# Modulation rows made inside the two expert loops, 512 columns per six tiles, instead of in the first stage, the merges, a projection and a feed-forward

## The reference, cut to what matters

```python
def first_block(...):
    c_act = jax.nn.silu(c)
    for l in range(2):
        mod = c_act @ ada_w[l] + ada_b[l]              # (D) @ (D, 6 D)
        sh_mix, sc_mix, g_mix, sh_ffn, sc_ffn, g_ffn = jnp.split(mod, 6, axis=-1)
        u = modulate(x, sh_mix, sc_mix)                # layer_norm(x) * (1 + sc) + sh
        ...                                            # w_in, four branches, gates
        x = layer_norm(DN_ALPHA * x + g_mix[:, None, :] * y, ln1_g[l], ln1_b[l])
        u = modulate(x, sh_ffn, sc_ffn)
        y = peer_ffn(u, ...)                           # the experts
        x = layer_norm(DN_ALPHA * x + g_ffn[:, None, :] * y, ln2_g[l], ln2_b[l])

def second_block(...):                                 # the same with c_2, ada_w_2, ada_b_2
    x = x + g_m * mixer(rms_norm(x) * (1 + sc_m) + sh_m)
    x = x + g_f * conv_ffn(rms_norm(x) * (1 + sc_f) + sh_f)
```

## Time and profile before

| what | value |
|---|---|
| device time, median of 3 runs | 4388.18 us (4385.45 to 4395.09) |
| profiled execution, span from first to last instruction | 4393.7 us |
| busy share of the span: PE, DVE, ACT, POOL | 79%, 62%, 42%, 4% |
| read from HBM | 633.94 MB, 145 GB/s over the span |
| mean granted PE clock | 0.896 |
| the two expert stages | 723.5 us each |
| the two merges | 188.5 us each |
| mod0 | 95.3 us |
| ffn_0 and ffn_1 | 267.2 and 207.7 us |

### The profile page before, as it was taken

How to read it: one execution, slowest core, us unless ns; L and a number is a source line. 1 busy time by engine, 2 the same in 40 slices (tenths; PEclk the granted TensorE clock), 3 DMA queues, 4 the chain that set the end, 5 groups by cost and what they waited for, 6 DMA issues and landing times. The chain is left out here.

```text
span 4393.7 us, 65322 instructions
## 1 busy us (share of the span) xinstructions
PE 3463.6 (79%) x20016; PEld 3012.6 (69%) x20016; DVE 2703.8 (62%) x5202; ACT 1834.7 (42%) x3304; POOL 154.6 (4%) x110
## 2 busy tenths in 40 slices
PE   1867865599999978678646999999674688796698
PEld 0846644589999968466445899999654577584587
DVE  6745648966666668456489666666634498344466
ACT  0433321755555544333218555555421234343244
POOL 0010000000000000100000000000003023000000
PEclk7978977899999989789778999999887799897799
DMA  7813621045555548136210455555410366451143
GB/s 257 277 51 106 218 99 57 19 148 188 185 190 187 186 154 268 52 116 225 90 48 19 158 187 186 190 188 185 174 52 25 135 235 215 143 184 34 55 180 129
DMA packets 279728, 636.50 MB, mean 145 GB/s; under 512 B 37896, under 2 KB 138896, under 8 KB 273472
## 3 DMA queue, kind: packets, MB, share of 16 engines
q1 hardware_dynamic: 279616, 635.15, 42.0%
HBM read 633.94 MB, written 1.15 MB: 145 GB/s over the span
## 5 line engine op out<-in xcount | busy, mean ns | idle before, releaser
L125 DVE TENSOR_TENSOR experts_u_lo<-u_w,experts_u_hi 128x512 fp32r<-128x512 f32 x512 | 353.8, 692 | 379.8 <-ACT experts_u_hi L122 379.8
L130 PE MATMUL experts_ps_h<-uP_hi,experts_u_hi 128*128 128x256 f32 x2048 | 576.9, 282 | 6.9 <-DVE experts_u_lo L125 6.9
L132 PE MATMUL experts_ps_h<-uP_hi,experts_u_lo 128*128 128x256 f32 x2048 | 574.5, 281 | 0.0
L131 PE MATMUL experts_ps_h<-uP_lo,experts_u_hi 128*128 128x256 f32 x2048 | 574.3, 280 | 0.0
L122 ACT ACTIVATE experts_u_hi<-u_w 128x512 fp32r<-128x512 f32 x512 | 323.1, 632 | 404.8 <-PE experts_ps_h L132 261.9
L125 DVE TENSOR_TENSOR experts_v_lo<-v_w,experts_v_hi 128x512 fp32r<-128x512 f32 x512 | 354.5, 692 | 179.8 <-ACT experts_v_hi L122 179.8
L122 ACT ACTIVATE experts_v_hi<-v_w 128x512 fp32r<-128x512 f32 x512 | 323.8, 632 | 233.2 <-PE expert_y L132 233.2
L130 PE MATMUL expert_y<-experts_v_hi,experts_w_hi 128*128 128x512 f32 x1024 | 405.2, 396 | 3.0 <-DVE experts_w_lo L125 3.0
L132 PE MATMUL expert_y<-experts_v_hi,experts_w_lo 128*128 128x512 f32 x1024 | 400.9, 391 | 0.0
L130 PEld LDWEIGHTS experts_ps_h<-uP_hi,experts_u_hi 128*128 128x128 f32 x2048 | 386.9, 189 | 17.1 <-issue 7.2
L131 PE MATMUL expert_y<-experts_v_lo,experts_w_hi 128*128 128x512 f32 x1024 | 397.9, 389 | 0.0
(11 more groups left out here) (516 smaller groups left out, 7614.3 us busy)
## 6 DMA issues: line engine op xcount, KB each, us to landing
u_w<-in_peer_u SPq DMA_DIRECT2D x256, 512.0 KB, 4.5
v_w<-in_peer_v SPq DMA_DIRECT2D x256, 512.0 KB, 3.3
up_w<-in_ffn_w_up SPq DMA_DIRECT2D x44, 1024.0 KB, 7.2
od_in_w<-in_od_w_in SPq DMA_DIRECT2D x36, 1024.0 KB, 5.1
in_w<-in_w_in SPq DMA_DIRECT2D x48, 752.0 KB, 5.4
merge_w_w<-in_w_gate SPq DMA_DIRECT2D x32, 1024.0 KB, 5.2
mod_mod_w<-in_ada_w_all SPq DMA_DIRECT2D x16, 1536.0 KB
in_proj_mod_w<-in_ada_w_all SPq DMA_DIRECT2D x24, 1024.0 KB
```

Of the source, the lines that this page charges most:

```text
L125: return dve.tensor_tensor(self.lo[at], value, self.hi[at].bitcast(F32), ALU.subtract)
L130: pe.matmul(out, left.hi[left_at], right.hi[right_at], start=start, stop=False, skip_group_check=skip)
L131: pe.matmul(out, left.hi[left_at], right.lo[right_at], start=False, stop=False, skip_group_check=skip)
L132: return pe.matmul(out, left.lo[left_at], right.hi[right_at], start=False, stop=stop, skip_group_check=skip)
```

## The change

The modulation rows are made elsewhere. Of row 0, `mod0` makes only the first 2048 columns, shift and scale of the mixer; the silu of both condition vectors is computed there once. `in_proj` of block 0 makes the next 3072 columns of row 0, as it made half of row 1 before. All else is made by a new class, `SpreadModulation`, in the two `experts` stages, in units of 512 columns. A unit takes six tiles: in each of the first four SP loads two chunks of 128 x 512 (512 KB) ahead of the tile's u load, and DVE adds the two chunks after the tile's own steps; in the fifth PE sums over the partitions; in the sixth ACT copies the row and stores it, from ACT's queue. The first `experts` stage makes 20 units (the last 1024 columns of row 0, all of row 1, half of row 3), the second 18 (row 2, the other half of row 3). `merge`, `in_proj` of block 1 and `ffn_0` make none; in `ffn_0` the low parts of the down weights are DVE's, as they were in `ffn_1`.

To know the row at build time, the loop over l is written out, so every stage of blocks 0 and 1 has its own code. The expert loop is unrolled by six tiles in place of two, in three hardware loops. Each norm loads and turns only its own 2048 columns, so the second norm of each block now does so as well. The gates are no longer loaded in the norms: `Residual`, `turn_project_add` and `conv_ffn` each load the one gate they use (512 KB) in their own stage; in `ffn_out` this load is the first of the stage, and DVE's first instruction needs it.

The core of the diff:

```diff
+class SpreadModulation:
+    CW = 512
+    def load(self, sync, unit, m, col, q):
+        at = bass.ds(col, self.CW)
+        if q == 0:
+            sync.wait_ge(self.ready, 1)
+            sync.wait_ge(self.added, unit * KD + 1)
+            sync.dma_start(self.bias[0:1], self.ada_b[m].unsqueeze(0)[:, at]).then_inc(self.bias_in, 16)
+        elif q >= 2:
+            sync.wait_ge(self.added, unit * KD + (2 * q - 1))
+        sync.dma_start(self.w[:, q % 2], rows_first(self.ada_w[m])[:, 2 * q:2 * q + 2, at]).then_inc(self.w_in[q % 2], 16)
+    def add(self, dve, unit, m, q):
...
+        for v in range(2):
+            k = 2 * q + v
+            if k:
+                dve.wait_ge(self.added, unit * KD + (k + 1))
+            dve.scalar_tensor_tensor(out=self.acc[:], in0=self.w[:, q % 2, v], scalar=self.silu[:, m // 2, k:k + 1],
+                                     in1=self.acc[:] if k else self.bias[:], op0=ALU.mult, op1=ALU.add).then_inc(self.added, 1)
+    def sum(self, pe, unit):
+        pe.wait_ge(self.added, unit * KD + (KD + 1))
+        pe.wait_ge(self.row_done, unit + 1)
+        pe.matmul(self.ps[0:1, :], self.ones[:], self.acc[:], start=True, stop=True).then_inc(self.summed, 1)
+    def keep(self, act, unit, m, col):
+        act.wait_ge(self.summed, unit + 2)
+        act.wait_ge(self.stored, unit * 16 + 16)
+        act.activation(self.row, self.ps[0:1, :], ACT.Copy).then_inc(self.row_done, 1)
+        act.wait_ge(self.row_done, unit + 2)
+        act.dma_start(self.mods[m].unsqueeze(0)[:, bass.ds(col, self.CW)], self.row).then_inc(self.stored, 16)
...
 def first_modulation
-        work = NextModulation(s, 4, 4, c_cols, ada_w, ada_b, row_out)
+        work = NextModulation(s, 1, 4, g.silu[:, 0], ada_w, ada_b, row_out, 0, 2 * D)
...
 def norm_turn
-                    sync.dma_start(mod.gate_mix[:], row_of(new_row[2 * D:3 * D])).then_inc(gate_in, 16)
-                    sync.dma_start(mod.gate_ffn[:], row_of(new_row[5 * D:6 * D])).then_inc(gate_in, 16)
-                    sync.wait_ge(gate_in, 32)
...
 class Residual
     def load(self, sync):
+        sync.dma_start(self.gate[:], row_of(self.gate_row)).then_inc(self.gate_in, 16)
...
     def vector(self, dve, link):
+        dve.wait_ge(self.gate_in, 16)
...
 def experts, SP
+                def loads(n, u, loads, unit, m, col):
+                    if m is not None and u < 4:
+                        work.load(sync, unit, m, col, u)
+                    sync.wait_ge(u_split, n * 2 + (2 - 2 * RING))
+                    pre.load(sync, n, u % RING, pre.sources)
...
 def experts, PE
+                    if m is not None and u == 4:
+                        work.sum(pe, unit)
...
 def experts, DVE
+                    if m is not None and u < 4:
+                        work.add(dve, unit, m, u)
...
 def two_blocks
+    spreads = ([(0, FFN_GATE, 2), (1, 0, 12), (3, 0, 6)], [(2, 0, 12), (3, 3 * D, 6), (None, 0, 2)])
-        with nc.Fori(0, DEPTH) as l:
+        for l in range(DEPTH):
```

More of the change, by code:

```diff
@@ L286, in _ @@
             def _(act):
-                work.begin_act(act)
+                act.wait_ge(c_in, 32)
+                act.activation(g.silu[:], c16[:], ACT.Silu).then_inc(silu_done, 1)
                 work.end_act(act, banks)
@@ L292, in _ @@
                 work.begin_vector(dve)
-                with dve.Fori(0, work.STEPS) as n:
-                    for u in range(0, work.PARTS, 2):
-                        work.accumulate_pair(dve, n, u)
+                dve.wait_ge(silu_done, 1)
+                for u in range(0, work.PARTS, 2):
+                    work.accumulate_pair(dve, 0, u)
             @block.tensor
@@ L315, in norm_turn @@
+MIX_COLS, FFN_COLS = 0, 3 * D
+MIX_GATE, FFN_GATE = 2 * D, 5 * D
+def norm_turn(nc, name, g, x, row, gain_cols, uP, uT=None, ahead=()):
     rms = gain_cols is not None
@@ L1446, in experts, with rounds @@
         ALL = slice(None)
+        units = sum(count for m, _, count in spread if m is not None)
+        assert sum(count for _, _, count in spread) == ROUNDS - 1 and NKEYS == RING + ROUNDS * ROUND and RING == 2
+        def rounds(engine, body):
+            done = 0
+            for m, first, count in spread:
+                with engine.Fori(0, count) as i:
+                    for u in range(ROUND):
+                        body((done + i) * ROUND + (RING + u), u, (done + i) * (ROUND // RING) + (2 + u // RING),
+                             done + i, m, i * SpreadModulation.CW + first)
+                done += count
         def each(engine, body):
             for u in range(RING):
-                body(u, u, 1)
-            with engine.Fori(1, ROUNDS) as i:
-                for u in range(RING):
-                    body(i * RING + u, u, i + 1)
+                body(u, u, 1, None, None, None)
+            rounds(engine, body)
+            for u in range(ROUND):
+                n = NKEYS - ROUND + u
+                body(n, u, n // RING + 1, None, None, None)
         with nc.Block() as block:
@@ L2218, in conv_ffn @@
         ps_u = s.ps("ps_u", [P, 2, 2, 512])
-        banks = [ps_u[:, part, v] for part in range(2) for v in range(2)]
         y = s.ps("y", [P, TB, D])
+        gate = s.sb("gate", [P, D])
+        gate_in = s.sem("gate_in")
         small_in, set_up, raw_done, cv_done = s.sem("small_in"), s.sem("set_up"), s.sem("raw_done"), s.sem("cv_done")
@@ L2226, in conv_ffn, with schedule @@
         hid_hi, hid_split = s.sem("hid_hi"), s.sem("hid_split")
-        def schedule(engine, steps, beside=None):
+        def schedule(engine, steps):
             for n in range(PEEL):
```

315 lines of the change are left out of this document (142 added, 173 removed).

## The result

The changed kernel takes 4239.69 us (median, 4235.21 to 4244.41), the kernel before 4388.31 us (4385.45 to 4395.09), both measured together: ratio 0.9658, 95% interval 0.9644 to 0.9673. The forecast was 4240.5. The profiled execution has a span of 4237.0 us against 4393.7, so 156.7 us less; the sum of the parts had said 147.7. The total is right, but its largest new cost is not, and errors of the other sign nearly cancel it.

The account below looks back on a forecast made before the run. The prediction took PE to bound the expert stage (718.6 of 723.5 us busy). Its terms summed to -147.7 us, taking the median from 4388.2 to 4240.5 us, with a range of 4215 to 4310 (the forecast's own 4222 to 4260).

Parts of the forecast that it names:

- The expert stages: Expert loops: PE gains 38 sums, paid in full, +33.6 us; copies, stores, adds and loads are covered.
- 0.885 each: Expert stages: price in us of one PE sum, from twelve records (six sums) taking 5.31 us at full clock.
- I count on one: Expert stages: u's load keeps some 1.4 us of slack, of 2.8, before PE wants it; one is relied on.
- the first rival: Expert stages: u lands over a us later in 152 tiles and PE waits; 76 us at 0.5 per tile, 4316; chance 0.18.
- The merges: Two merge stages: seven PE waits, some clock dips and the final sums go, 26 us each, -52 us.
- ffn_0: First feed-forward stage: without modulation work it becomes what ffn_1 is, 267.2 - 207.7, -59.5 us.
- mod0: First modulation stage: bytes fall from 25.2 to 8.4 MB, stage 45 us in place of 95.3, -50 us.
- the norms: Four norms before mixers lose the wait for gates, -20.3 us; with small costs in four other norms, -19 together.
- ffn_out: Start of ffn_out: DVE's first instruction waits for the gate load, 3.5 us, twice, +7 us; nothing hides it.
- The second: Merges: PE keeps waiting on the chain copy, low part, product; each gives 6 us, not 26; 4280 us, chance 0.10.
- The third: Expert loop: DMA engines set the pace, 40.6 us a round in place of 34.8; slower, 4428 us, chance 0.05.
- The fourth: Longer loops: instructions come late, say 1 us in each of 38 rounds, 38 us more; 4279 us, chance 0.05.

Follow-up runs that it names:

- the pad behind uP: The kernel before with 64 unused bytes per partition allocated behind uP, so every later tile lies 64 bytes further; 4399.65 us, ratio 1.0018.
- both pads: Two runs of the kernel before with 64 unused bytes per partition: allocated ahead of x and uP (4394.67 us), or behind uP (4399.65 us).

## Why the prediction held, point by point

*The expert stages, +33.6 forecast, +65.2 measured: the term that failed.* Two steps of it are at fault and one thing was not seen.

- "0.885 each", of which it said "below that the price cannot lie", was a lower bound taken as the value. Six sums in a row, as in the earlier trace rows, pay for the way in and out once for all six. A lone sum between other products pays it each time: 1.14 us, +9.7 over 38.
- "I count on one" microsecond of slack for u, and "I cost it at nothing". The landing was put at 3.3 + 1.9 = 5.2 us behind the issue of the modulation load. But 5.2 is u's median behind its own issue, which comes 0.68 us later:

```profile
1207.64 0.38 SPq L333 DMA_DIRECT2D experts_mod_w<-in_ada_w_all  x1
1208.32 0.33 SPq L109 DMA_DIRECT2D u_w<-in_peer_u  x1
```

In the 80 tiles with such a load u landed 6.2 us behind the issue of the modulation load in the median and 7.6 at the latest. So 1.0 of the 1.4 us of slack was gone in the median tile, and in the late ones all of it. PE lost 6.8 and 4.5 us, shown by reordering the queue. By the prediction's own mark (more than 5 us of PE's waits for experts_u_lo in a stage; 7.9 and 6.0) this is the first rival, real, but a seventh of its price: 11.3 us over 152 tiles are 0.07 us a tile, where the rival was priced at 0.5.
- Placement, 4.2 us a stage, was in no term: the text priced what the diff does to instructions, and a 64-byte tile moved others.

Together the first stage has 22.8 + 6.8 + 4.2 = 33.8 of its 35.8 us, the second 20.5 + 4.5 + 4.2 = 29.2 of 29.4. In the first some 1.4 us of the rest are one late product in the fourth tile of the first round of the new loop; which cause it has stays open. The prediction called itself wrong above 760 us for an expert stage, and the first stayed 0.7 us below that; the places that lost the rows shrank by 182 us, where it asked for 170.

*The merges, -52 forecast, -65.4 measured: right mechanism, too small.* The seven waits for modulation data went, and the two expected waits stayed (20.0 us, forecast 21). The tail was 6.2 by forecast; the stretch behind the last product fell from 10.8 to 3.6, so 7.2. The clock was mis-sized. At a mean of 0.92 the products ran 26.5 us at the lower level (1.2 GHz), which cost 13.3; at 0.97 over 140.2 us it is 8.4 us, which cost 4.2. So 9 were won, not 7, for the two waits that stayed leave less behind than was put down. 2.3 more are placement. Waits 33.6 - 20.0 = 13.6, clock 9, tail 7.2 and placement 2.3 are 32.1 of the 33.4.

*ffn_0, -59.5 forecast, -54.5.* The mechanism is exact: ffn_0 and ffn_1 now take the same, 212.7 and 212.1. The reference moved, because ffn_1 itself became 4.4 us longer. A little over half of that is placement: with silu behind uP, at the same granted clock of 0.95, they are at 209.9 and 209.5. The rest goes with the granted clock, which was 0.96 before. ffn_1 of the kernel without modulation loads, in the layout of the changed kernel, and of the kernel before with the pad behind uP, where 212 was expected:

```profile
4010.40:4219.60 209.20, 196.82 (x1328) 179.82 (x1328) 131.49 (x204) 95.46 (x155) 0.00 (x0) 0.97 0.40 146
```

```profile
4183.10:4392.30 209.20, 196.89 (x1328) 179.87 (x1328) 131.51 (x204) 95.55 (x155) 0.00 (x0) 0.97 0.39 144
```

Why the clock was lower in the changed kernel's ffn_1 stays open.

*mod0, -50 and -52.2; the norms, -19 and -20; ffn_out, +7 and +7.7; in_proj of block 1, -7.8 and -10.3.* As worked out. The norms before mixers, put at 14.8 each without a wait for gates, took 15.0, 15.0, 13.9 and 15.5. That in_proj of block 0 and the heads gain nothing was some 5 us short (-2.2, -1.7, -0.9).

*Terms of zero that were none.* qkv -5.8: placement, shown by the pad (-5.4). The two attends, -9.1 and -4.3: the trace shows where. The loop over l is written out, and the 32 loads of a bias table that begin the stage lost the address work that went with each (a MOVE at line 766 is part of it): they are issued 0.69 us apart, not 0.80. Before, and then after: the issues, the wait of POOL for the table, and PE's wait behind it.

```profile
276.42 25.62 SPq L766 DMA_DIRECT2D attend_nat_bias<-in_nat_rpb  x32
POOL attend_nat_bias L774 <- DMA attend_nat_bias<-in_nat_rpb: 33.8, 1, 33.8
PE attend_ps_p L814 <- ACT attend_prob L871: 7.0, 1, 7.0
```

```profile
217.62 22.04 SPq L810 DMA_DIRECT2D attend_nat_bias<-in_nat_rpb  x32
POOL attend_nat_bias L818 <- DMA attend_nat_bias<-in_nat_rpb: 29.4, 1, 29.4
PE attend_ps_p L858 <- ACT attend_prob L915: 1.1, 1, 1.1
```

The last issue ends 4.3 us earlier in the stage, and PE's wait is 5.9 us shorter in block 0 and 4.2 in block 1 (7.4 and 3.2), which there is nearly the whole gain. The rest of block 0 goes with its granted clock, 0.86 in place of 0.83. No run tests this alone. Under both pads, where the loop over l is as before, these stages kept their times (123.0 to 124.0).

Delta, -5.5, has the same code outside the loop and nearly the same waits of PE (29.6 and 29.1 us for its first load, then 14.4 and 11.0 both times), but a higher granted clock, 0.86 against 0.82 in this row of before:

```profile
3322.20:3445.40 123.20, 74.47 (x536) 71.22 (x536) 44.23 (x36) 24.90 (x33) 35.41 (x14) 0.82 0.06 22
```

It took 123.1 us under both pads, so it isn't placement. Why the clock fell less there stays open.

*The rivals.* The first is real and small, as above. The second is excluded: no merge is above 157. The third, DMA as the pace, is excluded, since the stages without modulation loads aren't shorter than those with u first. The fourth, late instructions, would show as a rest in every round; 2.0 and 0.2 us are left over 20 and 18 rounds. That total and forecast agree within 1 us is luck in two ways. Errors of +32 us in the expert stages and +9 in the feed-forwards stand against -13 in the merges, -19 in attends and delta, -6 in qkv and some -10 in small ones. And the spans differ by 156.7 us but the medians by 148.6, because the profiled span of before lay 5.4 above the median and that of after 2.7 below.

The Trainium skill's rule in "DMA: Bandwidth & Descriptors" (Measured, under Bandwidth), loads of 1 MiB or more for 75% of the peak, was held against this change. Here up to three loads of 512 KB a tile, 230 GB/s at a share of 0.68, were not what PE waited for once their order was right. Whether they would reach 75% of the peak no run here shows; the loop didn't need it.

## What to carry to other kernels

Work can be put into the cover of a PE-bound loop if what goes on PE itself is priced alone, between its neighbours, and not from a row of like instructions. A new load in a shared queue goes behind the load that is wanted next, not ahead of it: the bytes cost nothing, the place did. And where a change adds or resizes any tile, compare the start-to-start time of matmuls in stages that the change doesn't touch, before explaining their difference by contention. Where a hardware loop is written out, look at the queues too: loads issued one behind another can lose their address work and land earlier.

## What the hardware did that was not expected

- 64 bytes between the two operands of a matmul change its pitch: 24 products of 256 columns take 2.830 or 2.872 us, products of 512 columns start 235 or 227 ns apart, at the same granted clock. Two distances were compared, and in that pair the two widths want opposite ones. The layout with silu behind uP was good for both (2.827 us and 229 ns), and no run shows why.
- A plain fp32 matmul of 512 columns between split products costs 1.14 us where a second one behind it costs 0.86.
- DMA at a share of 0.67, in place of 0.53, adds nothing to a loop that PE bounds, if each load is issued in the order in which it is wanted (752.6 and 748.4 us with the loads, some 752.1 and 748.9 without).
